# A two-block transformer pair on one core: modulation strips spread over more places, low activations last in the first tiles of the output products, and a paired 512-wide first product in the second half of U

## The reference, cut to what matters

```python
# model 1, two layers (l = 0: gated linear attention; l = 1: sliding-window attention)
h = modulate(x, norm_g[l, 0], sh1, sc1);  x = x + g1 * mixer(h)
h = modulate(x, norm_g[l, 1], sh2, sc2);  x = x + g2 * peer(h)
# peer: per token 8 heads x 16 of 16384 single-neuron experts
q = h @ w_q;  e, g = top16 of sums of two 128-key scores, softmax
y = sum_e g_e * gelu(h . u_tab[e]) * v_tab[e]
# model 2, two layers (mLSTM, then MLA attention), each followed by an MLP
y = square(relu(h @ w1)) @ w2
# sh1, sc1, g1, sh2, sc2, g2 = silu(c) @ mod_w[l] + mod_b[l], in 28 strips of 1024 x 1024 over both models
```

## Time and profile before

| | |
|---|---|
| median of 3 runs | 2771.14 us (2770.6 to 2772.21) |
| profiled execution | 2766.39 us, span 2764.8 us, mean granted TensorE clock 0.977 |
| PE busy | 2624.3 us (95%), 18482 matmuls |
| DVE busy | 2089.8 us (76%) |
| ACT busy | 1145.6 us (41%) |
| POOL busy | 714.3 us (26%) |
| chain that ended last | PE 75%, DVE 11%, issue 6%, POOL 4%, DMA 2%, ACT 2% |
| HBM | 531.85 MB read, 194 GB/s over the span |

### The profile page before, as it was taken

The page is one execution under the profiler, slowest core; times in us unless marked ns, Lnnn a source line. Parts: engine busy times, 40 slices in busy tenths (PEclk is TensorE's granted clock), DMA queues, the critical chain, the costliest instruction groups (busy, mean ns, idle before and its releaser), DMA issues.

```text
span 2764.8 us, 51194 instructions
## 1 busy us (share of the span) xinstructions
PE 2624.3 (95%) x18482; PEld 2311.9 (84%) x18482; DVE 2089.8 (76%) x3398; ACT 1145.6 (41%) x1662; POOL 714.3 (26%) x461
## 2 busy tenths in 40 slices
PE   5989999999999999899999999999999899987998
PEld 4469999999877887789999998778888798866986
DVE  7545997777899778767987778997777798646890
ACT  1235444434434445434443334434445453322443
POOL 2001994000000000006980000000001085010787
PEclk9989999999999999999999999999999999998999
DMA  9634555444466876254555444667876446762454
GB/s 350 223 101 151 175 183 176 160 162 162 168 215 231 283 254 237 103 183 157 180 176 167 160 159 168 201 223 256 284 260 252 144 160 234 245 243 107 147 179 147
DMA packets 147627, 536.93 MB, mean 194 GB/s; under 512 B 16784, under 2 KB 17168, under 8 KB 147232
## 3 DMA queue, kind: packets, MB, share of 16 engines
q1 hardware_dynamic: 115088, 417.08, 44.7%
q0 software_dynamic: 31104, 113.26, 11.6%
q10 hardware_dynamic: 1296, 4.72, 0.4%
HBM read 531.85 MB, written 3.15 MB: 194 GB/s over the span
## 4 chain that ended last, share of the span: by engine, by line
PE 75%; DVE 11%; issue 6%; POOL 4%; DMA 2%; ACT 2%; DVEq 1%; SPq 0%; POOLq 0%; ACTq 0%
PE ps L1788 19%; PE ps L1401 15%; PE ps L1405 8%; PE ps L698 6%; PE ps L2494 5%; PE ps L1353 4%; POOL split_lo L1456 4%; PE ps L657 3%; PE ps L2476 3%; PE ps L1746 3%; PE ps L359 2%; DVE split_lo L1468 1%; PE ps L2480 1%; PE ps L635 1%; DMA ring<-in_stream 1%
## 5 line engine op out<-in xcount | busy, mean ns | idle before, releaser
L1443 ACT ACTIVATE split_hi<-ring 128x1024 fp32r<-128x1024 f32 x740 | 779.8, 1055 | 789.1 <-PE ps L1405 444.5
L1468 DVE TENSOR_TENSOR split_lo<-ring,split_hi 128x1024 fp32r<-128x1024 f32 x516 | 629.3, 1220 | 221.4 <-ACT split_hi L1443 221.1
L1456 POOL TENSOR_TENSOR split_lo<-ring,split_hi 128x1024 fp32r<-128x1024 f32 x208 | 551.5, 2669 | 172.1 <-ACT split_hi L1443 171.1
L376 POOL DMA_DIRECT2D mod_w<-in_mod x96 | 51.0, 531 | 1145.8 <-ACT gate L1498 426.5
L1401 PE MATMUL ps<-hT_hi,split_hi 128*128 128x256 f32 x2048 | 292.4, 285 | 0.0
L1405 PE MATMUL ps<-hT_hi,split_lo 128*128 128x256 f32 x2048 | 288.6, 284 | 2.5 <-POOL split_lo L1456 2.4
L1440 ACT ACTIVATE gate_hi<-gate 128x256 fp32r x256 | 106.9, 417 | 440.0 <-PE ps L1788 439.8
L1401 PE MATMUL ps<-hT_lo,split_hi 128*128 128x256 f32 x2048 | 287.4, 283 | 0.0
L1788 PE MATMUL ps<-split_hi,gate_hi 128*128 128x512 f32 x1024 | 284.1, 398 | 0.0
L1788 PE MATMUL ps<-split_hi,gate_lo 128*128 128x512 f32 x1024 | 276.3, 390 | 1.0 <-DVE gate_lo L1466 1.0
L1788 PE MATMUL ps<-split_lo,gate_hi 128*128 128x512 f32 x1024 | 276.6, 391 | 0.0
(11 more groups left out here) (383 smaller groups left out, 3886.0 us busy)
## 6 DMA issues: line engine op xcount, KB each, us to landing
ring<-in_stream SPq DMA_DIRECT2D x782, 512.0 KB, 4.1
mod_w<-in_mod POOLq DMA_DIRECT2D x96, 512.0 KB, 4.7
small<-in_mod POOLq DMA_DIRECT2D x80, 512.0 KB, 6.0
gate<-in_mod POOLq DMA_DIRECT2D x32, 512.0 KB, 9.2
gate<-in_mod ACTq DMA_DIRECT2D x8, 512.0 KB, 11.3
gate<-in_mod SPq DMA_DIRECT2D x8, 512.0 KB, 10.1
x_kept<-x POOLq DMA_DIRECT2D x4, 512.0 KB, 2.9
gate<-x_kept POOLq DMA_DIRECT2D x4, 512.0 KB, 9.1
```

Source lines behind the costliest of these rows:

```text
L1443: nc.scalar.activation(split_hi[:, e, :], ring[:, slot, e * D:(e + 1) * D], ACT.Copy).then_inc(hi_made, 1)
L1456: nc.gpsimd.tensor_tensor(split_lo[:, e, :], ring[:, slot, e * D:(e + 1) * D], split_hi[:, e, :].bitcast(F32), ALU.subtract).then_inc(lo_m ...
L1468: nc.vector.tensor_tensor(split_lo[:, e, :], ring[:, (START[name] + j) % RING, e * D:(e + 1) * D], split_hi[:, e, :].bitcast(F32), ALU.sub ...
```

## The change

It has five parts.

1. In the second half of U (32 slabs in each layer) `hT_lo` and `hT_hi` lie in one tensor `h_parts`, and one matmul of 512 columns takes w_hi against both: h_lo lands in columns 0 to 255 of a bank and h_hi in 256 to 511. The pass with w_lo stays 256 wide, onto columns 256 to 511. A bank now holds one tile. ScalarE copies the low halves of a slab's two banks to SBUF (`u_part`), VectorE adds the high halves (`u_sum_vector`), and ScalarE takes the Gelu from `u_part`. PE waits for the sum of the slab two before (`u_added`), and the start of V waits for the last sum.
2. `tile_gemm_M(last_by_tile=True)` takes in its first two tiles the four products with high activations first and the two with `yT_lo` last.
3. In all four mixers the gain row is stored before `turned_lo_vector`; in ml_out and mla_out it was stored at the end.
4. The chunks of the strips are spread: more of them stand ahead in the mixers, fewer behind the out product (swa, ml, mla). In mLSTM the head gains, the gating of the first token tile and the first `split_lo` of ml_out stand later. `Q_BANKS` of the query product is (2, 3, 6, 7) in place of (2, 3, 0, 1).
5. In both MLPs VectorE makes every `split_lo`, between its squares; GpSimd is left with the loads of the strips.

```diff
+            h_parts = scope.enter_context(nc.sbuf_tensor("h_parts", [P, 2, DC, SEQ], F32R))
+        hT_lo, hT_hi = h_parts[:, 0, :, :], h_parts[:, 1, :, :]
...
+            if last_by_tile:
+                for kind in (((split_hi, hi), (split_lo, hi)), ((split_hi, lo),)):
+                    for b in range(2):
+                        for w, src in kind:
+                            ready(b, w, src)
+                            for nb in range(nbs):
+                                for i in range(NT):
+                                    ins = product(b, w, src, 0, nb, i)
+                            if w is split_lo:
+                                ins.then_inc(lo_free, 1)
+                            elif src is lo:
+                                ins.then_inc(hi_free, 1)
...
-            turned_lo_vector(v, "gla.on", yT_lo, gla_y, bank=4)
             row_store(v, "g1_0", 0)
+            turned_lo_vector(v, "gla.on", yT_lo, gla_y, bank=4)
...
+            def paired_tile(i, j, e):
+                tile = first_tile + 2 * j + e
+                bank = (2 * j + e) % 4
+                t.eng.wait_ge(hi_made, i * 16 + (tile + 1))
+                for c in range(DC):
+                    nc.tensor.matmul(ps[:, bank, :].rearrange("p (a n) -> p a n", a=2), split_hi[:, e, c * P:(c + 1) * P],
+                                     h_parts[:, :, c, :], start=(c == 0), stop=False, skip_group_check=True)
+                t.eng.wait_ge(lo_made, i * 16 + (tile + 1))
+                for c in range(DC):
+                    ins = nc.tensor.matmul(ps[:, bank, SEQ:2 * SEQ], split_lo[:, e, c * P:(c + 1) * P], hT_hi[:, c, :],
+                                           start=False, stop=(c == DC - 1), skip_group_check=True)
...
+            def late_copy(i, j):
+                nc.scalar.activation(u_part[:, :, :], ps[:, bank:bank + 2, 0:SEQ], ACT.Copy).then_inc(u_copied, 1)
+            def late_gelu(i, j):
+                nc.scalar.activation(at(gate, i, 16 * SEQ, 2 * j * SEQ, 2 * SEQ),
+                                     u_part[:, :, :].rearrange("p a n -> p (a n)"), ACT.Gelu).then_inc(u_drained, 1)
+        def u_sum_vector(v, l, i, j):
+            nc.vector.tensor_tensor(u, u, ps[:, bank:bank + 2, SEQ:2 * SEQ], ALU.add).then_inc(u_added, 1)
...
-            t.eng.wait_ge(u_drained, (l + 1) * 68)
+            t.eng.wait_ge(u_added, (l + 1) * 32 + 2)
...
-        Q_BANKS = (2, 3, 0, 1)
+        Q_BANKS = (2, 3, 6, 7)
...
+            side_chunks_vector(v, "swa", 0, 2)      # ahead of the rotation of k
-            for n in range(6, 16):
-                if n < 12:
-                    less_splits_vector(v, "swa_out", n - 4, n - 3)
-                side_chunks_vector(v, "swa", n, n + 1)
+            side_chunks_vector(v, "swa", 10, 12)
+            for n in range(12, 18):
+                less_splits_vector(v, "swa_out", n - 10, n - 9)
+                if n < 16:
+                    side_chunks_vector(v, "swa", n, n + 1)
...
-            with v.eng.Fori(0, MLP_STEPS) as i:
+            for j in range(1, 4):
+                less(0, j, 0)
+                less(0, j, 1)
+                squares(0, j - 1)
+            with v.eng.Fori(1, MLP_STEPS) as i:
                 for j in range(4):
+                    less(i, j, 0)
+                    less(i, j, 1)
+                    if j:
+                        squares(i, j - 1)
+                    else:
+                        squares(i - 1, 3)
...
-            for n in range(15, 24):
-                if n < 21:
-                    less_splits_vector(v, "mla_out", n - 13, n - 12)
-                side_chunks_vector(v, "mla", n, n + 1)
-            post_rest_vector(v, "mla_out", 4, 0, "m2_1")
+            side_chunks_vector(v, "mla", 18, 20)
+            for n in range(20, 26):
+                less_splits_vector(v, "mla_out", n - 18, n - 17)
+                if n < 24:
+                    side_chunks_vector(v, "mla", n, n + 1)
+            v.wait_ge(vector_steps, v.n)
+            tile_post_vector(v, "mla_out", "m2_1", 0)
```

More of the change, by code:

```diff
@@ L713, in ready @@
                     t.wait_ge(*when((lo_mark if src is lo else hi_mark)(b * per + n)))
-            for b in range(tiles - (2 if last_by_tile else 0)):
+            if last_by_tile:
[10 more added lines that the diff above has]
+                                ins.then_inc(hi_free, 1)
+            for b in range(2 if last_by_tile else 0, tiles - (2 if last_by_tile else 0)):
                 for w, src in kinds:
@@ L801, in less_splits_vector @@
                 split_lo_vector(v, name, 0, b // 2, b % 2)
-        def splits_gpsimd(g, name, first, last):
-            g.eng.wait_ge(lo_made, TILE0[name] + first)
-            for b in range(first, last):
-                tile = TILE0[name] + b
-                g.eng.wait_ge(hi_made, tile + 1)
-                g.eng.wait_ge(lo_free, tile + 1)
-                nc.gpsimd.tensor_tensor(split_lo[:, b % 2, :], ring[:, (START[name] + b // 2) % RING, (b % 2) * D:(b % 2 + 1) * D],
-                                        split_hi[:, b % 2, :].bitcast(F32), ALU.subtract).then_inc(lo_made, 1)
         def half(nb):
@@ L1692, in routed_slab_vector @@
                 v.eng.wait_ge(u_drained, (l + 1) * 68 if odd else l * 68 + 4 + 32)
+            if not odd and not (first and j == 0):
+                u_sum_vector(v, l, i if j else i - 1, (j - 1) % 8)
             if j:
@@ L2428, in build, with ffn2_less_vector @@
         MLP_STEPS = FF // P // 8
-        FFN2_FIRST = 4
-        def ffn2_less_vector(v):
-            v.eng.wait_ge(lo_made, TILE0["ffn2_0"] + FFN2_FIRST)
-            for b in range(FFN2_FIRST, FF // P):
-                less_splits_vector(v, "ffn2_0", b, b + 1)
-                n = b - FFN2_FIRST
-                if n % 4 < 3 and n - n // 4 < DC * len(SIDE_STRIPS["f2_0"]):
+        def ffn2_less_vector(v, l, first, last):
+            for b in range(first, last):
+                less_splits_vector(v, f"ffn2_{l}", b, b + 1)
+                n = b - 4
+                if l == 0 and n >= 0 and n % 4 < 3 and n - n // 4 < DC * len(SIDE_STRIPS["f2_0"]):
                     side_chunks_vector(v, "f2_0", n - n // 4, n - n // 4 + 1)
@@ new lines, in less @@
+            def less(i, j, e):
+                tile = TILE0[f"ffn1_{l}"] + 2 * j + e
+                v.eng.wait_ge(hi_made, i * 8 + (tile + 1))
+                v.eng.wait_ge(lo_free, i * 8 + (tile + 1))
+                nc.vector.tensor_tensor(split_lo[:, e, :], ring[:, (START[f"ffn1_{l}"] + j) % RING, e * D:(e + 1) * D],
+                                        split_hi[:, e, :].bitcast(F32), ALU.subtract).then_inc(lo_made, 1)
+            for j in range(1, 4):
+                less(0, j, 0)
+                less(0, j, 1)
+                squares(0, j - 1)
@@ L2853, in _ @@
             for l in range(2):
[L2854 to L2862 removed]
+                side_loads_gpsimd(g, ("f2_0", "mla")[l])
         @block.scalar
```

114 lines of the change are left out of this document (71 added, 43 removed).

## The result

The changed kernel took 2737.81 us in the median of four executions (2732.97 to 2745.86) against 2771.68 us before. The ratio is 0.9875, with a 95% interval of 0.9846 to 0.9904: 27 to 43 us faster. The forecast was 2726 us with a range of 2713 to 2744. The direction and the range held, and 34 of the forecast 45 us came.

What follows compares the result with a forecast made beforehand. PE was taken as the bound, busy 95% of the span, with stalls between stages where VectorE is on the chain. Terms summing to -45.5 us took 2766.39 to 2720.9; plus 4.75 for the median, 2726 us, range 2713 to 2744.

Steps and rivals of the forecast that it cites:

- U: Second half of U: one 512-wide matmul every 0.228 us replaces two narrow ones at 0.240 a pair; -12.2 us.
- Rival A: U: the wide matmul costs two narrow ones, or the sum's order delays PE as much; 2738 us, chance 0.13.
- rival D: U's routed slabs: copy, sum and Gelu chain sets their pace, slower than before; 2800 us, chance 0.03.
- gla_out: Head of gla_out: gain row first and low activations last let PE start early at full pace; -5.4 us.
- Query product: Start of swa's query product: it now waits for banks 6 and 7, which VectorE frees later; +1.8 us.
- Tail of swa_out: From swa_out to peer_q1: fewer chunks behind the product, so VectorE is ready before it ends; -10.4 us.
- of mla_out: From mla_out to ffn1_1: three chunks fewer behind the product and the gain row gone from there; -9.5 us.
- rival B: Tails of swa_out and mla_out keep half their 20 us through half-pace sums or late loads; 2736 us, chance 0.12.
- mLSTM: Way to ml_out: values and gating earlier, split_lo and gain row added ahead of yT_lo; -0.8 us, between -3 and +1.5.
- MLPs: Both MLPs: without GpSimd's splits squares take 0.68 us and VectorE keeps up with PE; -8.0 and -3.3 us.
- rival C: MLPs: VectorE becomes the bound, with a slab above 5.66 us; 2748 us, chance 0.03.
- MLA: MLA mixer: moved chunks fall into VectorE's idle time; 1.5 us lost if a late load holds one before the scores.

Runs made afterwards that it cites:

- gla_row: Kernel before with only the gain row of gla_out stored ahead of the subtractions: 2773.55 us, ratio 0.9995.
- gla_both: Kernel before with only gla_out changed, gain row first and low activations last in the first two tiles: 2771.64 us, ratio 0.9997.
- no_fill: Changed kernel with old query banks, new order in gla_out alone, MLA's first chunks as before, and no 18 fillers behind swa_out: 2728.05 us, ratio 0.9839.
- best2: no_fill with the old order in gla_out too and V's strip chunks spread apart in its dense part: 2716.71 us, ratio 0.9797.
- u_only: Kernel before with only the pairing in the second half of U: 2763.67 us, ratio 0.9963.
- mlp_only: Kernel before with only all split_lo of both MLPs on VectorE: 2766.79 us, ratio 0.9972.
- again: The changed kernel measured once more, nothing edited: 2738.77 us, ratio 0.9885 against the kernel before.
- strips_only: Kernel before with only the strips of swa and MLA spread and the gain row of both stored first: 2760.12 us, ratio 0.9942.
- order_gla: Changed kernel with the new order of the first two tiles in gla_out alone, old order in the other three: 2730.62 us, ratio 0.9844.
- q_banks: Changed kernel with the query product of swa back in banks 2, 3, 0 and 1: 2731.23 us, ratio 0.9852.
- run 16: Not a follow-up run: a verb and a count, in the sentence saying TensorE had just executed 16 small sums; no kernel or time belongs to it.
- mla_chunks: Changed kernel with MLA's first strip chunks where they stood before: 2739.18 us, ratio 0.9872.

## Why the prediction came out as it did

The direction and the mechanism of the large terms were right, and the size of the sum was not: the two runs of the changed kernel won 33.9 and 35.0 us against the 45.5 of the sum. The terms as measured below add up to some 37; about 2 us of that the times don't show, less than V differs from trace to trace. What is missing lies in many small terms.

**U: -12.2 forecast, -10.9 measured** (209.54 to 204.10 us in each layer, rounded). The mechanism was right. The step that was mis-sized is the pace, 0.230 us a wide matmul in place of V's 0.228, and so 6.38 us a slab. The sum of two banks took 0.687 us, like the merge, and TensorE never waited for it. The wait ahead of V: +1.4 in both layers, forecast +1.3. Rival A, the wide matmul that pays nothing, is excluded: U fell in nine traces of nine. So is rival D: a slab took 6.38 us, far from 7.25. The rule of the Trainium skill ("TensorE: Matmul & The Clock Gate", section "Back-to-back issue gap") gave 2.6 us for this part (an estimate from that page), and these traces don't agree with it: 120 and 230 ns a matmul were measured where it gives 109 and 216. The page gives the rule for the gap of a matmul by itself, and here each matmul loads its own weights.

**gla_out: -5.4 forecast, -5.05 measured in the stage** (and not in the times of gla_row and gla_both), but with a wrong division. The prediction took the new order for what lets TensorE start before `yT_lo` is there. The row alone does it: TensorE's wait for it, for banks 0 and 1, was the whole wait, and behind it the low parts come in time one by one. The order costs its `split_hi` wait and wins nothing, here as in the other three products.

**Query product: +1.8 forecast, +2.2 measured**, undone by the old banks. The rotation's +0.5 can't be told: the stretch behind it runs from 72.0 to 75.5 us in the kernels with the old swa or only its strips moved and from 72.4 to 78.5 in the others.

**Tail of swa_out: -10.4 forecast, -9.3 measured** (15.7 us in six traces of seven with strips and fillers as in the change), **of mla_out: -9.5 forecast, -7.9 measured**. VectorE is ready ahead of time, as argued, and rival B's larger loss (half of both tails) didn't come. The step that was mis-sized is "PE still has 32 sums and 18 fillers, 5.8 us at full pace": the sums took 3.6 to 4.2 us and the fillers behind them ran at the low clock (4.19 us), some 8 us in all, and they became what is late next. Taking the fillers out behind swa_out gave 1.8 us. Behind mla_out the forecast was 15.8 us; it took 17.3 to 17.6, at a granted clock of 0.72 in the 12 us behind the product, and 15.9 in no_fill and best2, with the same fillers at 0.86, so there the clock is the whole of what was mis-sized.

**mLSTM: -0.8 forecast for way and product; -2 to -3.6 to the start of ml_out, and 0.3 to 1.6 back inside it.** Some 2 us in all on average, within the bounds. What came back inside ml_out is not the change's for the most part: it took 24.8 to 25.0 us also in u_only, mlp_only, gla_row and gla_both.

**MLPs: -8.0 and -3.3 forecast, -7.6 and -2.9 measured.** The first holds in all nine traces with this part, the second in five; three have -1.6 to -1.8 and again has -6.2. Squares of 0.68 us throughout, no wait in ffn2, and no bound by VectorE (rival C). GpSimd's splits had stretched the squares to 2.92 us; with them gone, 7.5 us of time in the run with this part alone. The trace agrees here with the Trainium skill ("SBUF — State Buffer", section "SBUF: two separate sides"), by which VectorE, when both its inputs come from SBUF, and a GpSimd instruction that reads SBUF take a shared port pair in turn, each for a whole instruction: that square began at 2266.22, GpSimd's split ran until 2268.60, and the square ended 0.54 us later.

**MLA: 0 forecast, +1.3 to +4.1 us measured** in four traces with these strips and the MLP part, but -1.1 in strips_only, and kernels with MLA as before run from 115.0 to 121.1 us. The step that failed is "The chunks moved into the mixer fall into VectorE's idle time". They did, but each used chunk releases the next load of 512 KB, and these loads fell into the stretch in which TensorE waits for its weights from the ring. The prediction had a price of 1.5 us for a chunk that comes late, and none for the weights that come late beside it. In the piece with the up-projection this shows as 1.8 us more idle time on average; 1.7 us more are clock, which also fell in four kernels with the chunks as before. mla_out itself took 0.5 to 2.1 us more, forecast +0.25; with the old order it ran from 22.2 to 23.8 us, so most of that is the clock again.

**The trace as a base.** The trace of before was a short one, 5 to 8 us below the medians of the kernel before in the runs, and the prediction added 4.75 for that. Part of the difference is V: 823.7 us is the shortest of all kernels with V as it was, whose mean is 830.4. Some stretches without a waiting transfer (the second half of U, MLP 0) repeat to 0.1 us from trace to trace.

Open are 5 to 6 us of the times of order_gla and of q_banks that their traces don't show, and the 5 us of gla_row and gla_both that the traces show and the times don't. Their intervals are 7 to 11 us wide, and V differs by as much from trace to trace without an edit.

## What to carry to other kernels

A step that is moved takes its transfers along (1 to 2 us here): look at the queue that its released slot feeds and at what else is loaded in that stretch, not only at the idle time of its engine. When a wait is taken away, name what its engine does itself in that gap (here fillers and small sums at the low clock), since that is what holds the path next. And look for what makes the same kernel's runs differ: here a double-buffered load with two uses in one step was worth about as much as the largest parts of the change (11 us between the medians of no_fill and best2), and no diff pointed to it.

## What was not expected of the hardware

The granted clock fell in the middle of V, in a stretch in which TensorE had stood still for 0.2 to 1.7 us now and then and had just run 16 small sums, in some traces and not in others, with the same instructions in the same order. The traces of before, after and mla_chunks have no such place in the dense part of V; gla_row has five, at 0.82 to 0.87 in windows of 6 us; at the price below they would be about half of the 15 us that its V has above that of before (an estimate). The same 6 us of layer 1's V in the windows of before and of again:

```profile
1815.59:1821.59 6.00, 6.00 (x48) 4.93 (x47) 3.65 (x9) 2.45 (x4) 0.00 (x0) 1.00 0.41 140
```
```profile
1800.04:1806.04 6.00, 6.00 (x21) 4.67 (x20) 2.89 (x8) 1.37 (x2) 0.00 (x0) 0.74 0.40 137
```

It costs 1.6 us (7.14 against 5.55 us from the first matmul behind the sums to the next routing group). What decides it, these traces don't show.

In one trace (again) all of ffn1_1 ran faster at a full clock: 708 matmuls in 80 us, against 682 in the same stretch of mla_chunks, 0.1135 us from start to start in place of 0.1175. It was worth 3.3 us, in that stage alone, and nothing in these traces says why.

```profile
2550.00:2630.00 80.00, 80.00 (x708) 80.00 (x707) 60.70 (x75) 38.88 (x45) 0.00 (x0) 1.00 0.60 197
```
```profile
2553.00:2633.00 80.00, 80.00 (x682) 80.00 (x680) 58.76 (x72) 36.80 (x43) 0.00 (x0) 1.00 0.59 190
```
